# A two-block transformer on one core: norm factors applied to the products, rotation by transfers

## What is computed

```python
def first_block(x, ...):
    h = rms_norm(x, attn_norm_w)
    z = h @ w_in                     # pool 512, q 1024, kv 768, gates 48, merge gates 2048
    q = rope(rms_norm(q, q_norm_w), pos) * SCALE      # 16 heads of 64
    k = rope(rms_norm(k, k_norm_w), pos)              # 3 branches x 2 groups
    y_pool = pool_mixer(u_pool) @ w_pool_br
    y_attn = nsa_attention(q, k, v, nsa_g) @ w_attn_br
    x = x + (merge_g[0] * y_pool + merge_g[1] * y_attn) @ w_o
    u = rms_norm(x, ffn_norm_w) @ w_up                # 2 x 2752, then a convolution of width 3
    return x + (silu(gate) * val) @ w_down

def second_block(x, ...):
    proj = rmsnorm(x, ln_mix_g) @ w_in                # neighbourhood attention and gated linear attention
    x = x + concat(y_na, y_gla) @ w_out
    x = x + square(relu(rmsnorm(x, ln_ff_g) @ w1)) @ w2
    return rmsnorm(x, ln_final_g)

rms_norm(x, w) = x * rsqrt(mean(x * x) + EPS) * w     # the mean over the 1024 features of a token
rope: (x1, x2) -> (x1 cos - x2 sin, x2 cos + x1 sin)  # x1, x2: the halves of 32 of a head
```

## Time and profile before

| | us |
|---|---|
| median of 3 runs (3470.49 to 3471.88) | 3471.28 |
| the profiled execution | 3471.35 |
| its span, first to last instruction | 3469.3 |
| TensorE busy | 3296.4 |
| VectorE busy | 1402.6 |
| ScalarE busy | 1276.0 |
| GpSimd busy | 268.8 |

### The profile page before, as it was taken

How to read it: one execution, slowest core, us unless ns; L and a number is a source line. 1 busy time by engine, 2 the same in 40 slices (tenths; PEclk the granted TensorE clock), 3 DMA queues, 4 the chain that set the end, 5 groups by cost and what they waited for, 6 DMA issues and landing times.

```text
span 3469.3 us, 40175 instructions
## 1 busy us (share of the span) xinstructions
PE 3296.4 (95%) x15554; PEld 2690.5 (78%) x15554; DVE 1402.6 (40%) x2292; ACT 1276.0 (37%) x1979; POOL 268.8 (8%) x459
## 2 busy tenths in 40 slices
PE   6999997899999998999999999999988899999998
PEld 4778886778888886888888877777866788888886
DVE  5432145655554334442442443365545422222223
ACT  4542135666666323221221222375613331313132
POOL 0000002333323200000000000110000000000000
PEclk9999997999999999999999999999988999999999
DMA  3111230000000321111111122100101111111111
GB/s 123 43 37 55 92 103 13 1 1 1 1 1 1 146 89 41 47 47 48 48 48 49 48 82 87 37 1 13 43 25 49 51 53 49 48 48 48 48 49 67
DMA packets 46239, 163.05 MB, mean 47 GB/s; under 512 B 6096, under 2 KB 7376, under 8 KB 45728
## 3 DMA queue, kind: packets, MB, share of 16 engines
q1 hardware_dynamic: 37152, 126.55, 11.5%
q0 software_dynamic: 8960, 34.77, 2.6%
HBM read 144.53 MB, written 16.78 MB: 46 GB/s over the span
## 4 chain that ended last, share of the span: by engine, by line
PE 90%; DVE 5%; ACT 3%; issue 2%; DMA 0%; POOL 0%; SPq 0%; ACTq 0%; DVEq 0%
PE PS L222 66%; PE PS L798 6%; PE PS L239 3%; PE PS L789 2%; PE PS L1440 2%; PE PS L1416 2%; PE PS L774 2%; PE PS L261 2%; PE PS L773 1%; PE PS L816 1%; PE PS L1429 1%; PE PS L808 1%; ACT QS L569 0%; PE PS L291 0%; PE PS L1722 0%
## 5 line engine op out<-in xcount | busy, mean ns | idle before, releaser
L195 ACT CAST WHI<-RAW 128x1024 fp32r<-128x1024 f32 x220 | 231.3, 1052 | 1629.3 <-PE PS L222 1598.8
L200 DVE TENSOR_TENSOR WLO<-RAW,WHI 128x1024 fp32r<-128x1024 f32 x220 | 269.4, 1225 | 1252.7 <-ACT WHI L195 1252.4
L222 PE MATMUL PS<-HLO,WHI 128*128 128x512 f32 x2176 | 671.4, 390 | 0.0
L222 PE MATMUL PS<-HHI,WHI 128*128 128x512 f32 x2048 | 641.8, 395 | 4.8 <-DVE W L1167 3.6
L222 PE MATMUL PS<-HHI,WLO 128*128 128x512 f32 x2048 | 631.4, 390 | 0.0
L222 PEld LDWEIGHTS PS<-HLO,WHI 128*128 128x128 f32 x2176 | 409.4, 188 | 85.9
L222 PEld LDWEIGHTS PS<-HHI,WHI 128*128 128x128 f32 x2048 | 383.7, 188 | 94.3 <-issue 9.9
L222 PEld LDWEIGHTS PS<-HHI,WLO 128*128 128x128 f32 x2048 | 385.1, 188 | 80.5
L222 PE MATMUL PS<-HID_HI,WHI 128*128 128x512 f32 x864 | 266.9, 390 | 2.1 <-DVE HID_LO L1176 2.1
L222 PE MATMUL PS<-HID_HI,WLO 128*128 128x512 f32 x864 | 266.4, 390 | 0.0
L222 PE MATMUL PS<-HID_LO,WHI 128*128 128x512 f32 x864 | 266.4, 390 | 0.0
(11 more groups left out here) (290 smaller groups left out, 4279.6 us busy)
## 6 DMA issues: line engine op xcount, KB each, us to landing
RAW<-in_w SPq DMA_DIRECT2D x220, 512.0 KB, 3.6
X<-in_x SPq DMA_DIRECT2D x8, 512.0 KB, 6.1
merged<-W POOLq DMA_DIRECT2D x8, 512.0 KB, 3.3
gate<-W POOLq DMA_DIRECT2D x8, 512.0 KB, 5.0
W<-gate POOLq DMA_DIRECT2D x8, 512.0 KB, 4.0
W<-merged POOLq DMA_DIRECT2D x8, 512.0 KB, 4.7
X<-in_x POOLq DMA_DIRECT2D x8, 512.0 KB, 9.4
x_kept<-X POOLq DMA_DIRECT2D x8, 512.0 KB, 8.4
```

The costliest lines, as they stand in the source:

```text
L195: nc.scalar.copy(WHI[:, slot, :], RAW[:, slot, :]).then_inc(w_hi, 1)
L200: nc.vector.tensor_tensor(WLO[:, slot, :], RAW[:, slot, :], WHI[:, slot, :].bitcast(F32), ALU.subtract).then_inc(w_lo, 1)
L222: last = nc.tensor.matmul(o[:, half], w[:, slot, cols], x(k)[:, half], start=(k == 0 and w is WHI and x is hi), stop=(k == kcs - 1 and w i ...
```

## The change

The normalisation factor of a token is the same for all features, so it can be applied after the product: `(x * w * r) @ W = ((x * w) @ W) * r`. The change does this for the norms 0 to 3:

- The row tile is weighted and split as soon as it is final, without the factor: `act_weighted_hi` and `dve_weighted_lo` replace `dve_norm` and `act_norm_hi`, in the load loop for norm 0 and in the residual loops for norms 1 to 3. There are separate HI tiles (`X_HI`) for the norms, and other buffers move to make room.
- `pe_mean` no longer stands ahead of `pe_first_units` but inside it, before tile 6 (norm 0) or tile 4.
- Every unit of a normalised stream is evacuated by VectorE, as PSUM times `RSTD` (`dve_scaled`, `dve_z2_unit`, `dve_ff2_up`), after the split of that step; sigmoid, silu, copies, the convolution and the square then read SBUF. ScalarE's waits move to `evacuated`.
- The matrix `ROTATE` and its matmuls go. `pool_rotate` issues four transfers of 32 partitions each on GpSimd's queue, which swap the halves of the heads within SBUF; the sign moves into `SIN`, two slices of which are negated once.
- The mean of the heads' squares is made of the rounded part and the rest of the squares (`SQ_HI`, `SQ_LO`) with a rounded `HM_R`, four matmuls of 512 columns in fp32r in place of the fp32 ones.
- SP loads the first constants, then weight and row tile by turns. The result of the pool part is split directly from PSUM.

```diff
@@ pe_first_units
+        hi = X_HI[n]
         for k in range(KC):
+            if k == (6 if n == 0 else 4):
+                pe_mean(pe, n)
             pe.wait_ge(h_ready, 8 * n + k + 1)
@@
+    def act_weighted_hi(act, n, k, x_k):
+        nc.scalar.activation(X_HI[n][:, k, :], x_k, ACT.Copy, scale=NORM_W[:, n, k:k + 1]).then_inc(hhi_done, 1)
+    def dve_weighted_lo(dve, n, k, x_k):
+        dve.wait_ge(hhi_done, 8 * n + k + 1)
+        nc.vector.scalar_tensor_tensor(HLO[:, k, :], x_k, NORM_W[:, n, k:k + 1], X_HI[n][:, k, :].bitcast(F32),
+                                       ALU.mult, ALU.subtract).then_inc(h_ready, 1)
+    def dve_scaled(dve, n, j, dst, more=0):
+        dve.wait_ge(job_done, j + 1 + more)
+        nc.vector.tensor_tensor(dst[:, :], PAIR[j % 2], RSTD[n][:, :], ALU.mult).then_inc(evacuated, 1)
@@ dve_z1_step
+        dve_split(dve, u + 2)
+        ...
+        dve_scaled(dve, 0, u, dst)
         if u - 2 in ROPE:
             dve.wait_ge(qn_done, r + 1)
-            dve.wait_ge(rot_done, r + 1)
-            seq(dve, nc.vector.tensor_tensor(ROPE_DST[r], W[4][:, :], COS[:, :], ALU.mult))
-            seq(dve, nc.vector.tensor_tensor(SIDE[1], SIDE[1], SIN[:, :], ALU.mult))
-            nc.vector.tensor_tensor(ROPE_DST[r], ROPE_DST[r], SIDE[1], ALU.add).then_inc(rope_done, 1)
+            dve.wait_ge(rot_done, 64 * (r + 1))
+            nc.vector.tensor_tensor(ROPE_DST[r], ROPE_DST[r], SIN[:, :], ALU.mult)
+            seq(dve, nc.vector.tensor_tensor(QN[:, :], QN[:, :], COS[:, :], ALU.mult))
+            nc.vector.tensor_tensor(ROPE_DST[r], ROPE_DST[r], QN[:, :], ALU.add).then_inc(rope_done, 1)
@@
+    def pool_rotate(pool):
+        for r in range(len(ROPE)):
+            pool.wait_ge(qn_done, r + 1)
+            for b in range(4):
+                pool.dma_start(ROPE_DST[r][32 * (b ^ 1):32 * (b ^ 1) + 32, :], QN[32 * b:32 * b + 32, :])\
+                    .then_inc(rot_done, 16)
@@ pe_z1_side
-            halves(pe, SIDE[1], ROTATE[:, :], W[4]).then_inc(rot_done, 1)
-            halves(pe, SIDE[0], HEADS_MEAN[:, :], W[2]).then_inc(ms_done, 1)
+            for src in (SQ_HI[r], SQ_LO):
+                for half in (slice(0, 512), slice(512, T)):
+                    last = nc.tensor.matmul(SIDE[0][:, half], HM_R[:, :], src[:, half], start=(src is not SQ_LO),
+                                            stop=(src is SQ_LO))
@@ act_z2
-                act.wait_ge(gl_k, 4 * (t // 2) + 4)
-                nc.scalar.activation(RG[t][:, :], src, ACT.Silu).then_inc(evacuated, 1)
+                act.wait_ge(evacuated, j + 1)
+                nc.scalar.activation(RG[u - U_RG][:, :], RG[u - U_RG][:, :], ACT.Silu).then_inc(rg_done, 1)
@@ dve_residual
             nc.vector.tensor_tensor(x[:, t, :], old(t), PAIR[j % 2], ALU.add).then_inc(evacuated, 1)
             dve_split(dve, u0 + t + 2)
+            if n < 4:
+                dve_weighted_lo(dve, n, t, x[:, t, :])
@@ dve_ff2_up
+        dve_split_at(dve, u + 2, more)
+        dve.wait_ge(job_done, j + 1 + more)
+        nc.vector.scalar_tensor_tensor(W[0][:, :], PAIR[j % 2], 0.0, RSTD[3][:, :], ALU.max, ALU.mult)\
+            .then_inc(evacuated, 1)
```

More of the change, by code:

```diff
@@ L297, in act_rstd @@
         act.wait_ge(ln_done, n + 1)
[L298 to L320, removed]
+        nc.scalar.activation(RSTD[n][:, :], LN_B[:, :], ACT.Exp, scale=-0.5).then_inc(rstd_done, 1)
+    def act_weighted_hi(act, n, k, x_k):
[7 more added lines that the diff above has]
+        nc.vector.tensor_tensor(dst[:, :], PAIR[j % 2], RSTD[n][:, :], ALU.mult).then_inc(evacuated, 1)
     ROPE = [U_Q + j for j in range(HPG)] + [U_KV, U_KV + 2, U_KV + 4]
@@ L326, in build @@
     ROPE_W = [QS_W[:, 0:1]] * HPG + [QK_W[:, 1 + b:2 + b] for b in range(3)]
+    ROPE_AT = [R + 4 * KB * j for j in range(HPG)] + [R + 40 * KB, R + 32 * KB, R + 36 * KB]
+    SQ_HI = [sb(f"SQ_HI{r}", [T], ROPE_AT[r], F32R) for r in range(len(ROPE))]
+    SQ_LO = sb("SQ_LO", [T], W_AT + 8 * KB, F32R)
+    QN = sb("QN", [T], R + 52 * KB)
     TURNED = [U_KV + 3, U_KV + 5, U_NSA]
@@ L354, in act_z1_step @@
             act.wait_ge(pool_mm, v + 1)
[L355 to L376, removed]
+            nc.scalar.activation(POOL_HI[:, v, :], SIDE[0], ACT.Copy, scale=POOL_SC[:, v:v + 1]).then_inc(pool_hi, 1)
         if u in ROPE:
             act.wait_ge(evacuated, u + 1)
+            if ROPE.index(u):
+                act.wait_ge(rst2_done, ROPE.index(u))
             nc.scalar.activation(W[2][:, :], W[u % 2][:, :], ACT.Square).then_inc(sq2_done, 1)
+            r = ROPE.index(u)
+            act.wait_ge(sq2_done, r + 1)
+            nc.scalar.copy(SQ_HI[r][:, :], W[2][:, :]).then_inc(sq2_hi, 1)
     def dve_window_sums(dve, g):
@@ L412, in dve_z1_step @@
     def dve_z1_step(dve, u):
-        if u < U_MIX:
-            dve_split(dve, u + 2)
+        dve_split(dve, u + 2)
+        dst = W[0] if u < U_Q else VCR if u == U_KV + 1 else W[u % 2]
+        i = sum(x <= u - 2 for x in TURNED)
+        if i:
+            dve.wait_ge(vt_done, i)
+        r = sum(x <= u - 2 for x in ROPE)
+        if r:
+            dve.wait_ge(qn_done, r)
+        if U_POOL < u <= U_Q:
+            dve.wait_ge(pooled_done, u)
+        dve_scaled(dve, 0, u, dst)
         if U_POOL <= u - 1 < U_Q:
@@ L1143, in act_ff1_conv @@
             act_split_at(act, u + b + 2, more)
-            act.wait_ge(job_done, jobs_before(u + b) + 1 + more)
+            act.wait_ge(evacuated, jobs_before(u + b) + 1 + more)
             if b == 0:
@@ L1998, in _ @@
     def _(dve):
-        for k in range(KC - 1):
-            dve_acc(dve, 0, k)
-        dve_split(dve, 0)
-        dve_split(dve, 1)
         dve.wait_ge(consts[0], 16 * N_FIRST)
         seq(dve, nc.vector.tensor_scalar(QS_W[:, :], QK_W[:, 0:1], -(HEAD ** -0.5), None, ALU.mult))
-        dve_norm(dve, 0, X)
+        for k in range(KC):
+            if k < 2:
+                dve_split(dve, k)
+            dve_weighted_lo(dve, 0, k, X[:, k, :])
+            if k < KC - 1:
+                dve_acc(dve, 0, k)
+        dve.wait_ge(rstd_done, 1)
         dve.wait_ge(consts[1], 16 * (len(const_loads) - N_FIRST))
+        for rows in (slice(0, 32), slice(64, 96)):
+            last = nc.vector.tensor_scalar(SIN[rows, :], SIN[rows, :], -1.0, None, ALU.mult)
+        seq(dve, last)
         for u in range(U_POOL, U_MIX):
```

285 lines of the change are left out of this document (155 added, 130 removed).

## The result

The changed kernel takes 3419.9 us (median of four runs, 3416.0 to 3421.6) against 3471.0 for the kernel before on the same chip: a ratio of 0.985, 95% interval 0.9838 to 0.9863. The forecast was 3419.6, range 3405 to 3443. A later set of four runs of the same kernel gave 3418.6 (3417.9 to 3423.3). That the total fits to 0.3 us is partly luck: the terms under it are off by up to 3 us each, and they cancel.

A forecast was written before the change was run, and what follows sets the result against it. TensorE, busy 3296 of 3469 us, was taken to bound the kernel. Start 14.0, means and rotation 27.8, later seams 21.9, less losses 12.0, gave 51.7 us off 3471.28: 3419.6 us, range 3405 to 3443.

The forecast's parts named there:

- Part 1, the start: Kernel start up to the first pooling product: first product at 11.5 us, pooling product at 45.4 against 59.4, gain 14.0.
- Part 2: Means and rotation of 11 head pairs: TensorE's 37.8 us of products become 10.0, gain 27.8 if the replacements are hidden.
- L: Time of the four POOL rotation transfers after the normalised tile QN: taken as 4.6 us, bounds 3.3 and 8.4.
- ring constant: Projection steps: the cycle QN, transfers, rotation, next QN takes 5.1 us plus L, against a step of 11.8.
- The 8 us per us of L: Eight back-to-back projection intervals: each us of L above 6.7 costs 8 us.
- Part 3, the seams: Three later places where a normalised stream begins: gains of 9.0, 6.0 and 6.9 us, together 21.9.
- Part 4, the losses: Evacuation by VectorE after its split, exposed at first FFN end, neighbourhood attention, attention start and gated linear attention: 12.0 us lost.
- Rival 1: Projection rotation a little late: L = 8.4 gives 3433 us, L of 10 gives 3450; chance 0.10.
- Rival 2: VectorE holds up POOL's issues of the rotation transfers: L = 7.9, +9 us, 3429; chance 0.06.
- Rival 3: The four rotation transfers land one after another: L = 13.2, +66 us, 3486; chance 0.05.
- three single rotations: Rotations outside the eight back-to-back intervals: each stalls TensorE by L less 6.7 and less 1.8 slack, 4.7 us each.
- Rival 4: Seams shrink less: last row splits queue, 3 us more each, slow clock returns, 1.9 each; +15, 3435; chance 0.10.

The follow-up runs named there:

- the second execution: The changed kernel, unedited, profiled a second time: span 3420.2 us, where its first profiled execution had 3414.2.
- the isolating runs: Changed kernel with rotation as a TensorE product again, 3440.3 us; with the heads' mean as an fp32 product of unrounded squares too, 3448.1 us.
- the serial run: Changed kernel with POOL waiting for each of the four rotation transfers to land before issuing the next: 3468.1 us.

## Why the prediction was right, point by point

- **What bounds the kernel.** Right: with 129 us more work on VectorE the time fell, and each step of the projections is exactly TensorE's list.
- **Part 1, the start.** 13.4 and 12.5 us in the two executions for 14.0. The first product came at 13.65, not 11.5. Two causes: the table load of 1.28, and my silent assumption that the second weight's split comes first once it has landed. It is queued behind the first row's work on both engines (its low part starts at 12.33 on VectorE). Of these 2.2 us 1.4 came back behind them: up to the end of the first of the paired units it took 25.8 us, where I had 25.9, but from there to the pooling product it is 6.6, where I had 8.0. I had put two table loads behind the mean product; the first runs at 26.32, during the products, and the factor is ready 3.5 us behind the mean and not 4.8.
- **Part 2.** 27.4 in the first and 28.4 in the second execution for 27.8; the isolating runs give 28.1 by the medians and 27.8 by the borders. L about 4.5 for the 4.6 taken, ring constant 5.0 for 5.1. The 8 us per us of L held up to 12.3.
- **Part 3, the seams.** 8.8, 5.3, 7.5 and, in the second execution, 4.9 for the last, for 9.0, 6.0, 6.9. The wait for the second unit's weight is there with its 2.5 us, but made of VectorE's sum of the last row (1.22) and the low part behind it (1.15); I had the cast and the low part, and the cast runs beside that sum. The slow clock behind it, which I priced at 1.9 a seam and left out, came at the third seam in one execution of two (1.6 us).
- **Part 4, the losses.** The end of the first FFN: the wait grew by 2.9 for the 2.4 forecast, and 1.6 came back at the head of that stage, where in before TensorE ran its first units slowly behind a wait of 3.6 us and now does not. Neighbourhood attention: 1.2 lost at its first scores (forecast 1.5), all but 0.1 regained later in the stage; why was not tested. Attention: 1.3 forecast, and nothing can be told from its spread. Gated linear attention: at its first scores 3.0 for 2.9, right; before the third scores 4.1 for 2.6, of which 1.6 is clock, so the list was right and the clock unpriced; at its end 1.5. Of this, 2.2 came back in the first execution behind the third scores, where TensorE's clock was higher than in before; in the second it did not.
- **The step that failed** is a judgement more than a number. I took the losses as the price of an evacuation on VectorE, with the split ahead of it as given. The runs show that exchanging these two operations wherever they stand together gives 20.7 us, more than the 12.0 of losses that I forecast, and that the stage which lost most is then no longer than in before.
- **Rivals.** Rival 1 did not come: L stays under 6.7. Rival 2: issues of 489 ns each (646 at most), the first two of the four beside a VectorE op with two SBUF inputs. In the serial run the first transfer of a head is issued at 141.72, inside SQ_LO (141.35 to 142.57), and lands 2.2 us later; the fourth, issued at 151.60 with VectorE idle, takes 2.2 as well. So VectorE held up neither issue nor landing. By the Trainium skill, "SBUF — State Buffer", section "SBUF: two separate sides", POOL's transfers starve beside VectorE ops in a two-port mode; no such stall shows in these rows. That section of the Trainium skill names the fp32 copy within SBUF as such an op, and nothing here shows that the ops in question run in that mode, so the rows don't speak against it; I had applied it too widely. Rival 3 does not describe the transfers as they are, and its price at L = 13.2 was too high in the term for the three single rotations. Rival 4: no wait for HLO inside the products.

## What to carry to other kernels

When a result moves to another engine, look at what stands ahead of it in that engine's list, and at what that in turn waits for: here a weight split needed 10 us later, and through it another engine's cast, stood ahead of a result needed at once. Where two units are made together tile by tile, let one of them begin and end alone, so that the other's weight and its own evacuation have cover. A pause of TensorE can cost more than its length, since the work behind it may run at the lower clock: here 1.6 us behind a pause of 2.5, in one execution of two.

## What the runs showed of the hardware

- Transfers between partitions of SBUF, issued by POOL: 128 KB alone landed 2.2 us after issue, four issued together in 2.7 (2.2 to 4.2), pieces of 32 KB in 1.7; each issue took 0.49 to 0.50 us. By the fit in the Trainium skill, "DMA: Bandwidth & Descriptors", section "Anatomy of one DMA — SWDGE (gpsimd) path", an estimate for 128 KB is 2.3, which the lone one bears out; the pieces of 32 KB, at 1.7, land sooner than the 2.0 that it gives as the fixed part.
- Beside a weight load they took longer. In the serial run the second transfer of a head took 4.7 us, in both rotations read one by one: SP had issued a 512 KB load 0.3 us before it, and its neighbours took 2.2. This is where the single long rotations can come from; no run moved the load to test it.
- TensorE's clock behind a pause differs between executions. Behind the 6.7 us wait for the transposed keys the next 24 products took 5.7, 6.6 and 7.4 us in executions of kernels with equal lists there; over the 12.5 us that begin with the scores in front of them the granted clock was 0.85 in the first execution of after and 0.66 in the second. Behind the 4.4 us that the exchanged order leaves, the products took 5.7 in both executions seen, but behind the 4.1 us of before they took 7.3, at 0.66:

```profile
2540.96 7.28 PE PS L222 x24
```

So a shorter pause does not by itself mean a higher clock behind it.
